# GpSimd makes ten low parts of weights at each boundary, and VectorE turns x's second group

## The reference

```python
for layer in range(DEPTH):                       # DEPTH = 2
    h = rms_norm(x, mix_pre_g[layer])
    m = pool_conformer_mixer(h, ...) if layer % 2 == 0 else short_conv_mixer(h, ...)
    x = x + rms_norm(m, mix_post_g[layer])
    h = rms_norm(x, ffn_pre_g[layer])
    x = x + rms_norm(sq_relu_mlp(h, ffn_w1[layer], ffn_w2[layer]), ffn_post_g[layer])
# then one hybrid layer: attention and spatial gating, merged, projected, added to x
```

## Time and profile before

| what | us |
|---|---|
| median of three runs | 2667.58 |
| the profiled execution, its own time | 2667.28 |
| its span, first to last instruction | 2665.5 |
| PE busy | 2660.2 (100%) |
| DVE busy | 1987.3 (75%) |
| ACT busy | 1286.8 (48%) |
| POOL busy | 278.7 (10%) |

### The profile page before, as it was taken

The page is one execution under the profiler, slowest core; times in us unless marked ns, Lnnn a source line. Parts: engine busy times, 40 slices in busy tenths (PEclk is TensorE's granted clock), DMA queues, the critical chain, the costliest instruction groups (busy, mean ns, idle before and its releaser), DMA issues.

```text
span 2665.5 us, 31068 instructions
## 1 busy us (share of the span) xinstructions
PE 2660.2 (100%) x11869; PEld 2204.6 (83%) x11869; DVE 1987.3 (75%) x2762; ACT 1286.8 (48%) x1609; POOL 278.7 (10%) x263
## 2 busy tenths in 40 slices
PE   9999999999999999999999999999999999999999
PEld 8888888888888888888888888888888888888887
DVE  6888877666766688777787676668668969985574
ACT  7776444444444454444544444344446545544452
POOL 4841100000000010000010000000011001000000
PEclk9999999999999999999999999999999999999999
DMA  8545655555655556565566555555555655565554
GB/s 265 182 174 196 212 192 189 190 189 194 205 186 190 201 179 218 195 198 192 187 203 199 198 190 188 191 190 196 190 191 184 210 174 176 178 215 189 190 205 143
DMA packets 268149, 515.58 MB, mean 193 GB/s; under 512 B 8498, under 2 KB 28260, under 8 KB 267492
## 3 DMA queue, kind: packets, MB, share of 16 engines
q1 hardware_dynamic: 267732, 513.34, 57.1%
q10 hardware_dynamic: 272, 0.26, 0.0%
HBM read 511.47 MB, written 2.10 MB: 193 GB/s over the span
## 4 chain that ended last, share of the span: by engine, by line
PE 99%; DVE 0%; ACT 0%; issue 0%; POOL 0%; DVEq 0%; POOLq 0%; ACTq 0%
PE bank L860 32%; PE bank L862 32%; PE bank L861 32%; PE bank L914 0%; PE bank L1113 0%; PE bank L996 0%; PE bank L999 0%; PE bank L1005 0%; DVE w_lo L843 0%; PE bank L931 0%; PE bank L1121 0%; DVE tap_product L2145 0%; PE bank L966 0%; DVE z L2133 0%; PE bank L1099 0%; PE bank L1130 0%
## 5 line engine op out<-in xcount | busy, mean ns | idle before, releaser
L843 DVE TENSOR_TENSOR w_lo<-w_raw,w_hi 128x1024 fp32r<-128x1024 f32 x946 | 1178.1, 1264 | 411.2 <-ACT w_hi L825 404.3
L825 ACT ACTIVATE w_hi<-w_raw 128x1024 fp32r<-128x1024 f32 x954 | 971.9, 1056 | 594.0 <-PE bank L862 408.1
L860 PE MATMUL bank<-w_hi,A_lo 128*128 128x512 f32 x2408 | 940.2, 390 | 0.1
L862 PE MATMUL bank<-w_hi,A_hi 128*128 128x512 f32 x2408 | 937.3, 389 | 0.0
L861 PE MATMUL bank<-w_lo,A_hi 128*128 128x512 f32 x2408 | 937.0, 389 | 0.0
L860 PE MATMUL bank<-w_hi,B_lo 128*128 128x512 f32 x1408 | 548.7, 390 | 0.0
L862 PE MATMUL bank<-w_hi,B_hi 128*128 128x512 f32 x1408 | 547.8, 389 | 0.0
L861 PE MATMUL bank<-w_lo,B_hi 128*128 128x512 f32 x1408 | 547.7, 389 | 0.0
L860 PEld LDWEIGHTS bank<-w_hi,A_lo 128*128 128x128 f32 x2408 | 452.1, 188 | 94.5 <-issue 1.6
L862 PEld LDWEIGHTS bank<-w_hi,A_hi 128*128 128x128 f32 x2408 | 452.0, 188 | 94.2
L861 PEld LDWEIGHTS bank<-w_lo,A_hi 128*128 128x128 f32 x2408 | 452.2, 188 | 93.1
(11 more groups left out here) (183 smaller groups left out, 1087.4 us busy)
## 6 DMA issues: line engine op xcount, KB each, us to landing
w_raw<-in_ffn_w SPq DMA_DIRECT2D x256, 1024.0 KB, 5.3
w_raw<-in_w_in SPq DMA_DIRECT2D x88, 1024.0 KB, 5.0
w_raw<-in_sc_w_in SPq DMA_DIRECT2D x48, 1024.0 KB, 5.1
w_raw<-in_ab_w_out SPq DMA_DIRECT2D x16, 1024.0 KB, 5.0
w_raw<-in_sc_w_out SPq DMA_DIRECT2D x16, 1024.0 KB, 5.0
w_raw<-in_w_out SPq DMA_DIRECT2D x16, 1024.0 KB, 5.1
w_raw<-in_ab_w_in SPq DMA_DIRECT2D x26, 512.0 KB, 4.8
w_raw<-in_ab_w_in SPq DMA_DIRECT2D x8, 1024.0 KB, 5.1
```

The source lines that it names most:

```text
L825: e.activation(w_hi[:, s % SPLIT_SLOTS, :], raw_step(s), ACT.Copy).then_inc(hi_made, 1)
L843: e.tensor_tensor(w_lo[:, slot, :], raw_step(s), w_hi[:, slot, :].bitcast(F32), ALU.subtract).then_inc(lo_made, 1)
L860: e.matmul(ps, lo[:, kt, tok], wh, start=first, stop=False)
L862: ins = e.matmul(ps, hi[:, kt, tok], wh, start=False, stop=last)
```

## The change

Ten of the steps behind each boundary (`POOL_STEPS`) get their low parts from POOL instead of DVE, by the same instruction, 128 x 1024, with two inputs in SBUF. Group 1 of x is turned by DVE in 16 transposes in one go, into a part of `conv_in`, and PE's eight transposes of it go. The steps at which groups 2 and 3 are turned and split move. ACT splits weights up to step 9 before it makes group 1's high part, and makes the statistics at steps 8 and 9 instead of 5. Step 3 is no longer halved. The waits on `lo_made` count only the steps that DVE splits (`LO_COUNT`), and PE and SP wait on `pool_lo` for POOL's.

```diff
-BY_VECTOR = (2, 3)
-X_TURNS = {2: (3, 5), 3: (8, 5)}
-X_HALVES = {2: 9, 3: 13}
+BY_VECTOR = (1, 2, 3)
+X_TURNS = {2: (5, 5), 3: (11, 4)}
+X_HALVES = {2: 10, 3: 15}
+POOL_STEPS = (3, 5, 6, 7, 8, 10, 12, 14, 16, 18)
...
-        HALVED = list(range(BEGIN)) + [S0[STAGE[p]] + n for p in range(1, 5) for n in (OPEN - 2, OPEN - 1)]
+        HALVED = list(range(BEGIN)) + [S0[STAGE[p]] + OPEN - 1 for p in range(1, 5)]
+        BY_POOL = [S0[STAGE[p]] + n for p in range(1, 5) for n in POOL_STEPS]
+        pool_lo = signal("pool_lo", [(s,) for s in BY_POOL])
+        LO_COUNT = [s + 1 - sum(b <= s for b in BY_POOL) for s in range(STEPS)]
...  (load_weights, SP)
-                    e.wait_ge(lo_made, STEPS_PER_LOAD * (n - RAW_SLOTS + 1))
+                    last = STEPS_PER_LOAD * (n - RAW_SLOTS + 1) - 1
+                    e.wait_ge(lo_made, LO_COUNT[last])
+                    if last >= BY_POOL[0]:
+                        e.wait_ge(pool_lo.sem, last + 1 - LO_COUNT[last])
...  (split_lo)
-                return
+            elif s not in BY_POOL:
+                split_lo_whole(e, s).then_inc(lo_made, 1)
+
+        def split_lo_whole(e, s):
             slot = s % SPLIT_SLOTS
             e.wait_ge(hi_made, s + 1)
-            e.tensor_tensor(w_lo[:, slot, :], raw_step(s), w_hi[:, slot, :].bitcast(F32), ALU.subtract).then_inc(lo_made, 1)
+            return e.tensor_tensor(w_lo[:, slot, :], raw_step(s), w_hi[:, slot, :].bitcast(F32), ALU.subtract)
...  (wait_step, PE)
+            elif s in BY_POOL:
+                e.wait_ge(pool_lo.sem, pool_lo.of(s))
...  (boundary, PE)
-                    if n == OPEN - 2:
-                        e.wait_ge(x_made.sem, x_made.of(p - 1, 1, 1))
-                        turn(lambda tt, part: x[:, tt, CH + part.start:CH + part.stop], "pre", p, 1)
...  (boundary, ACT)
-                split_to(e, split_hi, at, f + 6)
-                hi_x(p, 1)
+                split_to(e, split_hi, at, f + 9)
+                hi_turned(p, 1)
...  (boundary, DVE)
-                split_to(e, split_lo, at, f + 3)
                 update_first(p - 1, 1)
                 split_to(e, split_lo, at, f + 4)
+                update(p - 1, 1, 1)
                 lo_tile(p, 0, 1)
-                update(p - 1, 1, 1)
-                for tt in tiles:
-                    update(p - 1, 2, tt)
-                split_to(e, split_lo, at, f + 5)
+                e.wait_ge(x_made.sem, x_made.of(p - 1, 1, 1))
+                turn_blocks(e, x[:, :, CH:2 * CH], x_T[1], 0, 1).then_inc(x_turned(p, 1), 1)
+                update(p - 1, 2, 0)
+                lo_turned(p, 1)
+                update(p - 1, 2, 1)
                 for tt in tiles:
                     update(p - 1, 3, tt)
-                turn_x(p, BY_VECTOR[0], 0)
-                split_to(e, split_lo, at, f + 6)
-                lo_x(p, 1)
...  (finish, POOL)
-                e.wait_ge(lo_made, S0[STAGE[p + 1]] + 2)
+                f = S0[STAGE[p + 1]]
+                e.wait_ge(lo_made, LO_COUNT[f + 1])
                 gain(p, NG - 1, 0)
+                split(f + 3)
                 root(1, "postroot", "post", p, 1)
-                e.wait_ge(lo_made, S0[STAGE[p + 1]] + 5)
+                e.wait_ge(lo_made, LO_COUNT[f + 4])
                 gain(p, NG - 1, 1)
+                for n in POOL_STEPS[1:]:
+                    split(f + n)
                 root(NT, "rs", "pre", p + 1)
```

More of the change, by code:

```diff
@@ L604, in build @@
         FIRST_FILLS = AUX_N["ln", 0, 0]
-        SECOND = [("pre", p, 1, h) for p in range(1, 5) for h in two]
         def aux_bank(*key):
-            if key in SECOND:
-                key = ("pre", key[1], 0, 1, key[3])
             n = AUX_N[key]
@@ L613, in aux_free @@
         def aux_free(*key):
-            if key in SECOND:
-                return aux_done(("pre", key[1], 0, 1, key[3]))
             n = AUX_N[key]
@@ L624, in aux_free @@
                 return aux_done(aux[same[-1]])
-            before = aux[n - AUX_BANKS]
-            if before[0] == "pre" and before[2:4] == (0, 1):
-                before = ("pre", before[1], 1, before[4])
-            return aux_done(before)
+            return aux_done(aux[n - AUX_BANKS])
         tap_sums = [bank[7][:, 0:TOK], bank[7][:, TOK:2 * TOK]]
@@ L852, in step_matmuls @@
                 if s in HALVED and k == 1:
-                    e.wait_ge(lo_made, s + 1)
+                    e.wait_ge(lo_made, LO_COUNT[s])
                 kt = GK * ch.group0 + i * STEP_K + k
@@ L1200, in hi_plain, with statistics @@
                     e.activation(halves[buf][0][:, kt:kt + 2, :], view, ACT.Copy).then_inc(hi_cast(*key, h), 1)
-            def statistics(p):
-                for tt in tiles:
+            def statistics(p, which=tiles):
+                for tt in which:
                     if p == 0:
@@ L1234, in boundary @@
                 hi_tile(p, 0, 1)
-                split_to(e, split_hi, at, f + 6)
-                hi_x(p, 1)
+                split_to(e, split_hi, at, f + 9)
+                hi_turned(p, 1)
             def early(p, c, i):
                 n = POS[c, i] - S0[STAGE[p]]
-                if n == 5:
-                    statistics(p)
-                for g in BY_VECTOR:
+                if n in (8, 9):
+                    statistics(p, (n - 8,))
+                for g in BY_VECTOR[1:]:
                     if n == X_HALVES[g]:
@@ L1696, in early @@
                 at_step = POS[c, i] - S0[STAGE[p]]
-                for g in BY_VECTOR:
+                for g in BY_VECTOR[1:]:
                     if at_step == X_HALVES[g]:
                         lo_turned(p, g)
-                for g in BY_VECTOR:
+                for g in BY_VECTOR[1:]:
                     first, steps = X_TURNS[g]
                     n = at_step - first
-                    if (1 if g == BY_VECTOR[0] else 0) <= n < steps:
+                    if 0 <= n < steps:
                         turn_x(p, g, n)
@@ L2190, in gain, with split @@
                 e.tensor_tensor(out, out, gain_row[:, c], ALU.mult).then_inc(gained(p, n, tt), 1)
+            def split(s):
+                split_lo_whole(e, s).then_inc(pool_lo(s), 1)
             def finish(p):
```

5 lines of the change are left out of this document (3 added, 2 removed).

## The result

The changed kernel takes 2698.78 us (median of four runs, 2698.44 to 2701.12) against 2667.60 us for the kernel before, run beside it (2667.32 to 2667.70). The ratio is 1.0119, with a 95% interval of 1.0107 to 1.0131: 31.2 us slower. Forecast were 2690.5 us, with a range of 2670 to 2700 us. The time is in the range, 8.3 us from the forecast.

What follows compares the result with a forecast made beforehand. PE was taken as the bound, busy for all but 5 us. Per boundary 0.8 + 0.7 + 0.4 + 4.4 + 0.4 - 0.9 = 5.8 us, in all 23.2 on 2667.28: 2690.5 us, range 2670 to 2700.

Steps and rivals of the forecast that it cites:

- Step 2: At each boundary, POOL's split of step 3 holds DVE's split of step 2; PE waits 0.8 us.
- Step 4: DVE's finish, the mean and the update slip, so PE starts step 4 later; 0.7 us of it new.
- Tile 1: Group 1's update now stands ahead of the second lo_tile on DVE, so PE waits 0.4 us.
- item 4: At step 6, 16 DVE transposes, then lo_turned held by POOL's splits; PE waits about 4.4 us.
- rival A: POOL's split of step 10 doesn't slip between the two lo_turned; step 6 waits 2.2 us; 2681 us, chance 0.20.
- Step 16: At group 3, DVE's remaining work exceeds the time PE's steps leave it; 0.4 us, bounds 0 and 1.5.
- TensorE's transposes: PE's eight transposes per boundary go, saving 0.88 us each boundary, 3.5 us in all.
- rival C: PE's pause over 4 us at step 6 drops its clock; 9 us more, 2699 us; chance 0.14.
- a stretch of granted clock under 1.00: Sign in the profile after that the forecast is wrong because PE's pause costs clock.
- within 0.2%: Measured time not distinguishable from no change, 5.3 us; the prediction gave it a chance of about 0.16.
- Rival B: At the boundaries only DVE's splits are held, not SCALAR_TENSOR_TENSOR instructions; step 6's wait goes; 2673 us, chance 0.12.
- Rival D: POOL's splits don't hold DVE's where it matters, at step 2; only the 3.5 us gain remains; 2664 us, chance 0.08.

Runs made afterwards that it cites:

- the filled pause: The changed kernel with 16 extra matmuls, read by nobody, on PE ahead of step 6 at each boundary; 2691.07 us, ratio 1.0087.
- GpSimd's splits alone: The kernel before with only GpSimd's ten low parts added, x's groups turned as before; 2675.44 us, ratio 1.0029.
- the kernel with the zeros: The changed kernel with GpSimd filling its ten low parts per boundary with zeros instead of computing them; 2664.36 us, ratio 0.9988.

## Why the prediction was right, and where it was off

The direction, the mechanism and the places were right. By its own items:

1. **Step 2**, forecast 0.8 us: 0.61 to 0.65. GpSimd's split began 0.40 us ahead of VectorE's, forecast 0.4, and VectorE's took 3.07 us, forecast 3.1. With step 3 back on VectorE it is gone.
2. **Step 4**, forecast 0.7 us: 0.69. Same run, gone as well.
3. **Tile 1**, forecast 0.4 us: 0.37. But it is borrowed from item 4: with it taken away, item 4 grew by the same amount. The forecast added them, which was right for the sum (item 4 was worked out from a TensorE already that late), though not for what taking one away would give.
4. **Step 6**, forecast 4.4 us: 3.95 at boundaries 1 to 3, 3.79 at the fourth. Two of the four `lo_turned` are held, each by one GpSimd split, which rules out rival A. The turn's 7.16 us and GpSimd's splits of 2.4 us came as forecast.
5. **Step 16**, forecast 0.4 us: 0.55, and 0.1 more up to step 24.

TensorE's transposes gave 0.88 to 0.91 us (forecast 0.88). Without the clock these make 5.4 us per boundary, 21.5 in all, where 23.2 were forecast.

The term that was mis-sized is the clock, in the sum at zero and in rival C at 9 us with a chance of 0.14. It fell behind each of the four pauses of 3.6 us and more, to 0.51 in the fourth boundary's window; the landmarks give 8.9 us, the filled pause 7.7. So the forecast's waits came, and rival C's clock with them, which is C's case with its time of 2699 us: a stretch of granted clock under 1.00 is what the prediction itself named as its sign of being wrong in favour of C. That 2698.8 us lies within the range is owed to C at the range's upper end.

I set C's chance low on a misreading. The prediction says that no row of the kernel before has the lower level, but its last microsecond has. TensorE's last matmul there starts at 2661.87 us and ends at 2662.26. Windows of the kernel before:

```profile
2663.00:2664.50 1.50, 0.00 (x0) 0.00 (x0) 0.05 (x1) 0.00 (x0) 0.00 (x0) 1.00 0.51 172
2664.50:2665.50 1.00, 0.00 (x0) 0.00 (x0) 0.00 (x0) 0.00 (x0) 0.00 (x0) 0.59 0.01 4
```

So the trace did show the clock fall, between 2.2 and 3.3 us after TensorE stopped, and a pause of over 4 us was forecast. The Trainium skill (TensorE: Matmul & The Clock Gate, HAM oscillation), cited there for the slower case, was right here: the clock fell, and the kernel with the filled pause shows that the pause is the cause. The size of C's term, 9 us for 8.9, has luck in it. It took the lower level to last as long as a pause of 4.4 us; the pauses were of 3.6 to 3.8 us, and TensorE worked at the lower level for 3.1 to 5.7 us. Windows of the change at the second boundary, and then at the fourth:

```profile
973.80:974.80 1.00, 0.97 (x4) 0.86 (x5) 1.00 (x3) 0.00 (x0) 0.00 (x0) 1.00 0.00 0
974.90:978.20 3.30, 3.30 (x9) 2.60 (x8) 3.26 (x7) 2.00 (x2) 0.00 (x0) 0.50 0.00 0
978.30:982.00 3.70, 3.70 (x18) 3.07 (x17) 3.59 (x8) 3.50 (x4) 2.36 (x1) 1.00 0.48 130
...
2036.40:2037.40 1.00, 0.00 (x0) 0.03 (x1) 1.00 (x2) 0.00 (x0) 0.57 (x1) 0.50 0.00 0
2037.40:2043.10 5.70, 5.70 (x14) 4.50 (x15) 5.61 (x11) 2.15 (x3) 0.00 (x0) 0.50 0.00 0
```

At the fourth boundary the clock is down before TensorE resumes at 2037.40; at the second it falls a microsecond after TensorE has resumed at 973.83. At the four boundaries in turn 7, 8, 12 and 13 matmuls ran at the lower level, each some 0.2 us longer from start to start. That is the 1.59, 1.70, 2.74 and 2.82 us.

One slip in the chances: D and half of B make 0.14 for "within 0.2%", not 0.16.

Rival B, that only splits are held, is refuted three times over: `update` 3.00 instead of 0.75 us, and four `lo_turned` 5.61 us in the change and 3.82 with GpSimd's splits alone, instead of 1.68. Rival D's condition, no hold where it matters, is what the kernel with the zeros makes true, and it came to D's 2664 us.

Not settled: why the lower level lasts longer at some boundaries than at others behind nearly the same pause. The order of the boundaries does not decide it: with step 3 on VectorE the cost is 2.97, 1.72, 1.55 and 2.84 us.

## What to carry to other kernels

A second engine's work is free only beside instructions that don't want the same thing: before you move a two-tensor instruction to GpSimd, write down what VectorE does in each of its microseconds, and put it beside transposes and reads of PSUM, not beside other two-tensor instructions. Count a hold in whole instructions of the other engine (2.4 us here for a 0.48 us one). When a forecast contains a pause of TensorE of some microseconds, add the clock to the sum as a term, or fill the pause; and check that no gain rests on two engines' starts being apart by less than a tenth of a microsecond.
